# Running sums of the stick-breaking attention as two fp32r products, split on VectorE

## The reference

```python
z = einsum('bthd,bshd->bhts', q_b, k_b) * scale
log_1m = where(strict, log_sigmoid(-z), 0.0)           # strict: s < t
acc = lax.cumsum(log_1m, axis=3, reverse=True) - log_1m  # running sum over s
w = where(strict, exp(log_sigmoid(z) + acc), 0.0)
out = einsum('bhts,bshd->bthd', w, v_b)
```

## Time and profile before

| | |
|---|---|
| median of 3 runs | 983.71 us (982.79 to 984.46) |
| the profiled execution: its time, and its span from first to last instruction | 982.79 us, 981.1 us |
| TensorE (PE) busy | 963.4 us, 98% |
| VectorE (DVE) busy | 680.2 us, 69% |
| ScalarE (ACT) busy | 619.4 us, 63% |
| GpSimd (POOL) busy | 333.7 us, 34% |
| chain that ended last, by engine | PE 82%, POOL 7%, DVE 5%, issue 4% |

### The profile page before, as it was taken

One profiled execution on the slowest core, in us unless ns is written; L12 is line 12 of the kernel. 1 busy time (PEld: TensorE's weight loads), 2 busy tenths in 40 slices (PEclk: granted clock), 3 DMA queues, 4 the chain that ended last, 5 costly groups with the idle time before them and its releaser, 6 DMA issues.

```text
span 981.1 us, 19103 instructions
## 1 busy us (share of the span) xinstructions
PE 963.4 (98%) x6234; PEld 876.3 (89%) x6234; DVE 680.2 (69%) x1377; ACT 619.4 (63%) x1026; POOL 333.7 (34%) x152
## 2 busy tenths in 40 slices
PE   8999989999999999999999999999999999999998
PEld 5887879999999999999999998888888888888877
DVE  6636663999935888888888884666655555667663
ACT  6477554266665888888888885555555555566643
POOL 0002020088887777777777773000000000012000
PEclk9999999999999999999999999999999999999999
DMA  8563422045554444444444445555567777555511
GB/s 313 215 221 122 174 89 87 1 151 181 183 181 167 168 159 164 164 157 171 152 169 158 163 163 181 193 192 193 193 234 236 236 251 230 194 194 192 191 61 43
DMA packets 43803, 168.94 MB, mean 172 GB/s; under 512 B 5075, under 2 KB 6524, under 8 KB 42492
## 3 DMA queue, kind: packets, MB, share of 16 engines
q1 hardware_dynamic: 43392, 168.46, 49.5%
q10 hardware_dynamic: 380, 0.07, 0.0%
HBM read 167.45 MB, written 1.06 MB: 172 GB/s over the span
## 4 chain that ended last, share of the span: by engine, by line
PE 82%; POOL 7%; DVE 5%; issue 4%; ACT 1%; DMA 1%; POOLq 0%; SPq 0%; DVEq 0%; ACTq 0%
PE pair L1410 12%; PE pair L1407 12%; PE pair L1409 12%; PE bank L1119 11%; PE bank L1121 11%; PE bank L1120 11%; POOL t_lo L1082 7%; PE pair L1369 3%; PE pair L1144 2%; PE pair L1145 2%; PE pair L1146 2%; DVE w_lo L667 1%; PE pair L1450 1%; PE pair L1452 1%; PE pair L1451 1%
## 5 line engine op out<-in xcount | busy, mean ns | idle before, releaser
L1082 POOL TENSOR_TENSOR t_lo<-t_raw,t_hi 128x1024 fp32r<-128x1024 f32 x130 | 312.3, 2412 | 153.0 <-ACT t_hi L519 152.9
L519 ACT ACTIVATE t_hi<-t_raw 128x1024 fp32r<-128x1024 f32 x256 | 270.5, 1057 | 80.1 <-DMA t_raw<-v_chunks 56.0
L1119 PE MATMUL bank<-xt_hi,t_hi 128*128 128x256 f32 x1024 | 290.1, 283 | 2.0 <-POOL t_lo L1082 2.0
L1120 PE MATMUL bank<-xt_lo,t_hi 128*128 128x256 f32 x1024 | 289.8, 283 | 0.0
L1121 PE MATMUL bank<-xt_hi,t_lo 128*128 128x256 f32 x1024 | 289.8, 283 | 0.0
L820 DVE TENSOR_TENSOR t_lo<-t_raw,t_hi 128x1024 fp32r<-128x1024 f32 x126 | 154.7, 1228 | 100.1 <-ACT t_hi L519 99.9
L1407 PE MATMUL pair<-t_hi,g_hi 128*128 128x512 f32 x512 | 199.2, 389 | 0.0
L1409 PE MATMUL pair<-t_lo,g_hi 128*128 128x512 f32 x512 | 199.2, 389 | 0.0
L1410 PE MATMUL pair<-t_hi,g_lo 128*128 128x512 f32 x512 | 199.2, 389 | 0.0
L1119 PEld LDWEIGHTS bank<-xt_hi,t_hi 128*128 128x128 f32 x1024 | 196.5, 192 | 2.4 <-POOL t_lo L1082 2.4
L1120 PEld LDWEIGHTS bank<-xt_lo,t_hi 128*128 128x128 f32 x1024 | 196.6, 192 | 0.0
(11 more groups left out here) (246 smaller groups left out, 1304.4 us busy)
## 6 DMA issues: line engine op xcount, KB each, us to landing
t_raw<-u_chunks SPq DMA_DIRECT2D x128, 512.0 KB, 3.3
t_raw<-v_chunks SPq DMA_DIRECT2D x128, 512.0 KB, 3.3
w_raw<-w_in SPq DMA_DIRECT2D x4, 2048.0 KB, 8.4
w_raw<-w_query SPq DMA_DIRECT2D x4, 2048.0 KB, 7.7
w_raw<-w_in SPq DMA_DIRECT2D x8, 512.0 KB, 8.8
w_raw<-w_out SPq DMA_DIRECT2D x2, 2048.0 KB, 7.8
wg_raw<-w_gate SPq DMA_DIRECT2D x8, 512.0 KB, 4.7
h<-x SPq DMA_DIRECT2D x2, 512.0 KB, 4.3
```

The lines of the kernel that those rows point to most:

```text
L519: nc.scalar.activation(t_hi[:, q % RING, :], t_raw[:, q % RING, :], ACT.Copy).then_inc(t_hi_ready, 1)
L1082: nc.gpsimd.tensor_tensor(t_lo[:, q, :], t_raw[:, q, :], t_hi[:, q, :].bitcast(f32), ALU.subtract).then_inc(t_lo_pool, 1)
L1119: mm(dst, ah, bh, start=(c == 0), stop=False)
L1120: mm(dst, ah, bl, start=False, stop=False)
```

## The change

The softplus is split into two fp32r tensors, and the running sum is made of both. VectorE copies triangle and ones once to fp32r (`tri_r`), then for each e, once GpSimd has masked it, rounds the softplus to fp32r (`sp_hi`, a cast that lies where `sb_w` lies) and subtracts that from the softplus (`sp_lo`, in place of `sb_sp`). TensorE runs the five products of `running_sum` once with `sp_hi` and once with `sp_lo`. The two casts, two subtractions and the copy stand ahead of `value_out(1, 1)` on VectorE, and `split_group(6)` now stands behind it.

```diff
+        sp_hi = tile("sp_hi", [P, 2, 1536], ZONE + 4 * 8192, f32r)
+        sp_lo = tile("sp_lo", [P, 2, 1536], ZONE + 4 * 5120, f32r)
+        tri_r = tile("tri_r", [P, 2, P], ZONE + 4 * 4096, f32r)
...
             value_out(1, 0)
+            nc.vector.tensor_copy(tri_r[:, :, :], cst[:, 1:3, :]).then_inc(tri_ready, 1)
+            for e in range(2):
+                dve.wait_ge(sp_masked, e + 1)
+                nc.vector.tensor_copy(sp_hi[:, e, :], sb_sp[:, e, :]).then_inc(sp_split_hi, 1)
+                dve.wait_ge(sp_split_hi, e + 1)
+                nc.vector.tensor_tensor(sp_lo[:, e, :], sb_sp[:, e, :], sp_hi[:, e, :].bitcast(f32),
+                                        ALU.subtract).then_inc(sp_split_lo, 1)
+            value_out(1, 1)
             split_group(6)
-            value_out(1, 1)
...
             def running_sum(e):
-                pe.wait_ge(sp_masked, e + 1)
-                lower, upper = sb_sp[:, e, 0:1024], sb_sp[:, e, 1024:1536]
...
+                tri, ones = tri_r[:, 0, :], tri_r[:, 1, :]
+                for k, half_of, ready in ((0, sp_hi, sp_split_hi), (1, sp_lo, sp_split_lo)):
+                    pe.wait_ge(ready, e + 1)
+                    lower, upper = half_of[:, e, 0:1024], half_of[:, e, 1024:1536]
+                    for b in range(2):
+                        mm(bank[3 * e + b][:, :], tri, lower[:, 512 * b:512 * (b + 1)], start=False, stop=False,
+                           skip_group_check=True)
+                        mm(bank[3 * e + b][:, :].rearrange("p (i t) -> p i t", i=2)[:, :, P:SEQ], ones,
+                           upper[:, 256 * b:256 * (b + 1)].rearrange("p (i t) -> p i t", i=2), start=False,
+                           stop=(k == 1), skip_group_check=True)
+                    ins = mm(bank[3 * e + 2][:, :], tri, upper, start=False, stop=(k == 1), skip_group_check=True)
+                ins.then_inc(cum_done, 1)
+
+            pe.wait_ge(tri_ready, 1)
             running_sum(0)
```

More of the change, by code:

```diff
@@ L220, in layer_program @@
         z_done, z_softplus, sp_added, sp_masked = sem("z_done"), sem("z_softplus"), sem("sp_added"), sem("sp_masked")
+        tri_ready, sp_split_hi, sp_split_lo = sem("tri_ready"), sem("sp_split_hi"), sem("sp_split_lo")
         cum_done, w_exp, w_masked = sem("cum_done"), sem("w_exp"), sem("w_masked")
```

## The result

The changed kernel takes 994.28 us (median of 4 runs, 993.88 to 995.11) beside 984.09 us for the kernel before: a ratio of 1.0103, 95% interval 1.0091 to 1.0115. It is slower by about 10.2 us. The sign was forecast; 986.7 us and a range up to 988.5 us were not near. The profiled execution took 995.11 us with a span of 993.4 us, 12.3 us more than the span of the one before: 10.2 us of it are there when the output projection starts, and most of the rest comes from a second low stretch of the clock near 150 us, which lasted 6.8 us here and 3.4 us in the trace before.

A forecast was written before the change was run, and what follows sets the result against it. VectorE's second bias pair bounds the kernel: 5.73 us added + 1.22 turns + 0.48 standing - 4.45 idle used = 2.98 us later; on the 983.71 us median, 986.7 us, range 984.9 to 988.5 us.

The forecast's parts named there:

- The sign: Whole kernel: slower than before, chance 0.73; no difference 0.24, faster 0.03.
- TensorE's side: Running sums: fp32r products at 0.23 and 0.12 us save 1.58 us for each e, 3.2 us in all, spent waiting.
- Prices on VectorE: Split on VectorE: two subtractions 3.51 us, two casts 1.93 us, one small cast 0.29 us; 5.73 us added.
- The turns: VectorE's split and GpSimd's second masks exclude each other: 1.22 us of turns plus 0.48 us of standing.
- Rival 1: VectorE and GpSimd do not take turns at the split: 1.47 us later, 985.2 us; chance 0.15.
- A shift passes through whole: Behind the output projection's start at 113.50 us all is one chain, so the 2.98 us delay reaches the end.
- rival 3: TensorE's clock falls in the new holes, 93.8 to 99.2 us: +1.0 us, 987.7 us; chance 0.12.
- nothing else is late: Besides VectorE: TensorE finishes round 1's scores at 93.8 us, four us before VectorE wants them; SP and ScalarE have room.
- Rival 4: The clock's fall near 140 us goes away: -1.3 us on the forecast, 985.4 us; chance 0.08.
- Rivals 2 and 5: 2: split's casts take 1.76 us each, 988.3 us, chance 0.07. 5: split hidden, TensorE's saving counts, 980.7 us, chance 0.03.

The follow-up runs named there:

- e3_products_only: Changed kernel without VectorE's split: the softplus add writes fp32r, both rounds of fp32r products read it, VectorE's order as before; 984.25 us, ratio 0.9998.
- e1_fill: Changed kernel with 21 more fp32r products of 512 columns, results thrown away, in TensorE's three holes; 985.4 us, ratio 1.002.
- e6_fill_one: Changed kernel with 10 fp32r products of 512 columns in the last hole only, behind round 2's scores; 986.95 us, ratio 1.002.
- e12_fill_half: Changed kernel with 5 instead of 10 added products in the last hole only; 985.83 us, ratio 1.0022.
- e7_fill_late: Changed kernel with 16 fp32r products of 512 columns behind the transposes at 98.3 us, not in the hole; 992.32 us, ratio 1.0077.
- e2_split_only: Changed kernel with running sums in fp32 as before, the split written where nobody reads; 994.32 us, seven executions 992.48 to 996.90, three 984.76 to 987.33.
- e5_again: The changed kernel once more, no edit; 995.25 us.
- e9_before_fill: Kernel before with only 10 fp32r products added near 138 us, between the second norm's two groups of transposes; 982.2 us, ratio 0.9987.
- e4_reorder: Changed kernel with weight rest of group 6 behind the third maximum and subtraction, group 7's behind the transposed low halves; 983.64 us, ratio 0.9997.
- e10_fp32_best: Kernel before with both weight rests late, second value copy early, 4 products behind round 2's scores, fill near 138 us; 982.63 us, ratio 0.9989.

## Why the prediction was wrong

- *TensorE's side*: right. 0.23 and 0.12 us a product, 3.2 us saved, and the saving spent on waiting (e3_products_only finds nothing of it in the time).
- *Prices on VectorE*: right. The casts took 1.38 and 0.95 us, the subtractions 2.06 and 1.76 us; forecast were 0.96 and 1.76 us and turns with GpSimd on top.
- *The turns*: right in kind, too dear. The small copy, the first cast and the first subtraction stood for 0.42, 0.43 and 0.30 us, 1.15 us in all against 1.22 + 0.48 = 1.70 us. Rival 1, no turns at all, is refuted. Besides, the copy began at 81.58 us and instructions that don't wait for each other overlap by some 0.08 us. The second subtraction ended at 88.35 us instead of 89.09 us, value copy and weight rest took 4.85 instead of 5.02 us, bias to bias 3.72 instead of 3.81 us. That is the whole difference between 2.98 us and the measured 96.92 - 94.95 = 1.97 us.
- *"A shift passes through whole"*: right within the noise. With the holes filled (e1_fill) the projection is 1.92 us late and the three kernels whose last hole is filled (e1_fill, e6_fill_one, e12_fill_half) have medians 1.3, 2.3 and 2.2 us above the kernel before beside them. This term alone lies about at the bound of 0.2%.
- *The step that failed is rival 3's price*, and with it the sentence that nothing else is late. The mechanism stood there: TensorE's clock falls in the new holes, with 1.1 of 5.4 us of work (measured: 1.14 of the 4.96 us from 93.29 to 98.25 us). It was given 0.12 and a price of +1.0 us, at most 1.9 us, for which the prediction shows no working. That is about what a low stretch as short as the one in the trace before would cost; that one lasted 3.4 us (0.66 on average over 5 us). The new one lasted 20.5 us in both traces of the changed kernel, through the first transposes, all the value products and nearly all of the next transposes (L1282).
- *That price by what is read now* starts from the transposes in the trace before:

```profile
96.53 1.06 PE L1238 MATMUL pair<-cst,s 128*128 128x128 f32 x8 [0.77 <-ACT s L446]
```

  From these transposes to the output projection the kernel before needs 113.50 - 96.53 = 17.0 us, the changed one 123.71 - 98.25 = 25.5 us. That is 8.5 us, and with 1.7 us of later start the 10.2 us.
- *What is shown of its cause, and what isn't.* That the last hole makes the fall is shown by e1_fill, e6_fill_one and e12_fill_half, 28 executions with it filled or half filled and none near 994 us. Why it lasted so long is shown only in part. Light work stands behind this hole, and with 16 dense products behind it the long stretch was gone (e7_fill_late). But the work alone doesn't set the length. Seventeen low stretches stand in the traces of all runs, apart from the last microseconds of a span, and only three lengths occur: ten lasted 3.4 us, five 6.8 us and two 20.5 us. Light work followed the two long ones and also one of the 3.4 us (e2_split_only); at the place of the earlier trace rows, where dense fp32r products of 256 columns follow, the clock was low for 3.4 us in five traces and for 6.8 us in five others, with both lengths for the changed kernel.
- *The chance* was wrong for the same reason. The holes were worked out, found emptier than the stretch in which the clock was seen to fall, and then given one in eight. The changed kernel was hit in eight of eight executions.
- *Rival 4*, that the fall near 140 us goes away, did not happen by itself: it came again near 150 us, for 6.8 us in the first trace and for 3.4 us in the second (e5_again), as long as before. Filled, that hole is worth 1.4 us (e9_before_fill).
- *Rivals 2 and 5* are refuted by the casts' 0.95 us and by VectorE's row without a gap.

What stays open: what decides between a low stretch of 3.4, 6.8 and 20.5 us; why e2_split_only is hit for long in seven executions and for a short time or not at all in three, while the changed kernel, whose last hole is no longer but has two others ahead of it, is hit in all eight; and what ended the low stretch of the changed kernel at 116.8 us, under transposes, and at 119.0 us in the second trace, under value products. No run was made for any of them.

## What to carry to other kernels

- A longer wait of TensorE can cost several times its length. Here a hole grew from 0.8 to 2.6 us, the granted clock fell to half, and 8.5 us were lost in the work behind it. Look in the stretches for any place where the granted clock has fallen, but don't price a new hole by the length of that one stretch: the long one, 20.5 us, was seen only where transposes and fp32 products of 64 columns stood behind the hole, and with dense fp32r products behind it none of the traces shows more than 6.8 us.
- Before adding work to an engine that is waited for, look down its row for something that is wanted much later. Here 4.4 us of weight rest, moved behind the scores, made room for the whole split (e4_reorder). Where nothing has to be fitted in, the same move gains nothing (e10_fp32_best).
- Where a hole can't be closed, a few products into a bank that nobody reads then can keep the clock: in e1_fill, e6_fill_one, e12_fill_half and e9_before_fill the clock stayed at 1.00 where it had fallen before, and TensorE's next work started no later.

## What the runs showed of the hardware that was not expected

- The low clock lasted 20.5 us while the profile had TensorE busy for 5.00 of 5 us in three stretches running; under 16 fp32r products of 512 columns it ended after 3.4 us. Busy time in the profile says little about whether the clock comes back, and under the same light work it came back after 3.4 us in the trace of e2_split_only.
- The same program is hit or not from one execution to the next (e2_split_only: 984.76 to 996.90 us), which makes two groups of times and not a spread. Part of the spread of every kernel here is of this kind: the kernel before has 982.5 us with a mean clock of 0.998 and 986.6 us with 0.995.
- VectorE's instructions and GpSimd's masks delayed each other: VectorE's stood for about 1.15 us here, less than the 1.70 us worked out. As in the earlier trace rows, an instruction stands only for what is left of the other engine's.
